# A decoder step on one core: two projections moved into the norm stage, one split around a product

## The chip, the cores and the metric
One Trainium2 chip, one of its cores. The metric is the time of one execution in microseconds (us) on the device, median of several runs. TensorE is called PE here, with PEld for its weight loads; VectorE is DVE, ScalarE is ACT, SyncE is SP (it issues most DMAs), GpSimd is POOL.

## The reference, cut to what matters
One layer of a decoder runs on 1024 prompt rows and 64 sampled rows (8 sequences of 8), each 1024 wide:

```python
h = rms_norm(x, norm_attn)
proj = h @ w_in                       # columns: x_r | q | k | v | gate a | gate b, each 1024 wide
x_c = causal_dwconv(x_r, ...)         # width 4
y_a = rg_lru(x_c, ...)                # gates, decay, a scan over positions
lam = exp(sum(lq1*lk1)) - exp(sum(lq2*lk2)) + lambda_init
# per head: w = softmax(q1 k1^T/8 + bias) - lam * softmax(q2 k2^T/8 + bias);  o = w v
y_b = rms_norm(o, subln_g) * (1 - lambda_init)
x = x + (sigmoid(g_a)*y_a + sigmoid(g_b)*y_b) @ w_out
h2 = rms_norm(x, norm_ffn)
x = x + (gelu(conv(h2 @ w_up)[:, :3072]) * conv(...)[:, 3072:]) @ w_down   # conv of width 3
y = rms_norm(x, norm_final)
```
The bias of a head depends only on the distance between query and key. The rows of K and V and several states are outputs too. Everything is float32; each large product is made of three products of rounded parts (high by high, high by low, low by high).

## The kernel before, in words
The program has four stages, one after another: `front`, `heads`, `sampled_and_out`, `mixer`. Each is a block in which every engine has its own list of instructions, tied together by semaphores. A block ends when all engines are through their lists; only then does the next one start.

**`front` (lines 88 to 361)** works on nine tiles of rows (eight of 128, one of 64). For each tile ACT sums squares and takes the root (`ssq`), DVE scales (`gain`), PE transposes eight 128x128 pieces into PSUM (`tile`, line 212), ACT writes the high part `h_hi` (`high`, 267), DVE the low part `h_lo` (`low`, 324). Transposes of tile t wait for `low` of tile t-2. Between tiles PE does four small things: transposes of parameter rows `prow` (222), three products that make the bias rows (229), one that spreads lambda over the partitions (234), and after tiles 6, 7 and 8 transposes of the mixer's parameter rows `frow` (244). DVE copies the bias rows to SBUF (343), SP writes them to DRAM (186). When ACT has done the high parts of the K and Q weights of head 0 (279), it issues two DMAs from DRAM to DRAM that lay these rows out as tiles: head 0 (283) and heads 1 to 7 (286). SP loads the weight slices `w_raw` of head 0 (180): K and Q behind all of x, V and XR behind the write of the bias rows.

**`heads` (445 to 1227)** runs over eight heads. All engines follow one list, `TURN` (364): each engine does its own part of every entry. `("P", g, c)` is the projection of group g (XR, K, Q, V, gates) for column chunk c (384, 384 and 320 columns): 24 matmuls (line 1152); `QK` are the scores, `SA`, `EX`, `SB` the softmax, `TW` transposes of the weights, `PV` the product with V (1220), `SQ` and `SS` the head's norm, `TR` transposes of K or V rows for the outputs (1179), `G..` the recurrent branch, `FA`, `FG` the merge. `P`, `TR`, `TW` and `G` results share three PSUM banks as a ring, taken in the order of `TURN`: an entry waits until the one three places before it has been released by ACT or DVE. `SA` of query block 0 needs the bias tile: SP waits for DMA 283, then loads it (693). At the start of the stage ACT and DVE split the V weights (711, 898), compute decay rates, split the XR weights, and split the small gate weights `rg_raw`, which SP loads at the stage's start (639).

PE's stage code ends a head with:
```python
("GAM",), ("P", GB, 1), ("P", GB, 2), ("TR", V_, 2), ("TW", 7, 0), ("TW", 7, 1), ("W", Q_, 1), ("TR", K_, 2),
("PV", 3), ("SQ", 3), ("FA",), ("SS", 3), ("FG",),
```
`("PV", 3)` is the last product with V; ACT then squares it (871) and copies it (872), and `("SQ", 3)` is PE's sum of the squares (1226).

Of the kernel before, what the change touches and what calls it, by code (L numbers as in the profile page):

```python
# [21 lines left out]
H, HD = 8, 64  # L22
# [64 lines left out]

def front(nc, sb, sem, ins, c):
# [13 lines left out]
    lam = sb("lam", [1, 4, HD], F32)  # L102
    lprod = sb("lprod", [1, 2, HD], F32)
    lsum = sb("lsum", [1, 2], F32)
    lexp = sb("lexp", [1, 2], F32)
    ltmp = sb("ltmp", [1, 2], F32)
    ones_row = sb("ones_row", [1, 128], F32)
# [29 lines left out]
    s_lsum = sem("s_lsum")  # L137
    s_lexp = sem("s_lexp")
    s_nl = sem("s_nl")
    s_nlb = sem("s_nlb")  # L140
# [6 lines left out]
    with nc.Block() as block:  # L147
        @block.sync
        def _(sp):
# [3 lines left out]

            load_x(0)
            sp.dma_start(g[:, :], broadcast_row(ins["norm_attn"], 128)).then_inc(g_in, 16)
            sp.dma_start(c.ptab[:, :], ins["page_table"].rearrange("(o b) n -> o (b n)", o=1)).then_inc(ptab_in, 16)
            for i, name in enumerate(("lambda_q1", "lambda_k1", "lambda_q2", "lambda_k2")):
                sp.dma_start(lam[:, i, :], ins[name]).then_inc(lam_in, 16)
# [8 lines left out]
            sp.dma_start(prow[r:r + n, :], flat(ins["state_rglru_conv"])).then_inc(prm_in, 16)  # L167
            load_x(3)
# [7 lines left out]
            sp.dma_start(frow[0:FCONV_W, :], flat(ins["ffn_conv_w"])).then_inc(frow_in, 16)  # L176
            sp.dma_start(frow[FCONV_W:FCONV_W + 1, :], flat(ins["ffn_conv_b"])).then_inc(frow_in, 16)
            sp.dma_start(frow[FCONV_W + 1:FROW, :], flat(ins["state_ffn_conv"])).then_inc(frow_in, 16)
            def load_w(grp):
                sp.dma_start(c.w_raw[:, W_SLOT[grp], :, :], c.w_in[:, :, COL0[grp]:COL0[grp] + 128])\  # L180
                  .then_inc(c.raw_in[W_SLOT[grp]], 16)

            load_w(K_)
            load_w(Q_)
            sp.wait_ge(rows_sb, 1)
            sp.dma_start(c.bias_rows_dram, bias_rows[:, :]).then_inc(rows_out, 16)
            load_w(V_)
# [4 lines left out]
            sp.wait_ge(rows_out, 16)  # L192
# [11 lines left out]
        def _(pe):  # L204
            def tile(t):
                n, u = rows(t), t % 2
                pe.wait_ge(xn_done, t + 1)
                for q in range(2):
                    if t >= 2:
                        pe.wait_ge(lo_done, 2 * (t - 2) + q + 1)  # L210
                    for k in range(4):
                        last = pe.transpose(ps[:, 2 * u + q, 128 * k:128 * k + n],
                                            xn[0:n, u, 512 * q + 128 * k:512 * q + 128 * (k + 1)],
                                            c.ident[0:n, 0:n])
                    last.then_inc(xt_done, 1)

            pe.wait_ge(id_done, 1)
            tile(0)
            tile(1)
            pe.wait_ge(prm_in, 16 * 7)  # L220
            for k in range(KT):
                last = pe.transpose(ps[:, 4, NROW * k:NROW * (k + 1)], prow[:, 128 * k:128 * (k + 1)],
                                    c.ident[0:NROW, 0:NROW])
            last.then_inc(prm_t, 1)
            tile(2)
            pe.wait_ge(tab_in, 32)
            pe.wait_ge(fills, 3)
            for i in range(3):
                last = pe.matmul(ps[0:H, 5 + i, 0:UW], rel[:, :], oh[:, UW * i:UW * (i + 1)],
                                 start=True, stop=True)  # L230
            last.then_inc(rows_mm, 1)
            tile(3)
            pe.wait_ge(s_nl, 1)
            pe.matmul(ps[:, 4, 480:481], ones_row[:, :], ltmp[:, 1:2], start=True, stop=True).then_inc(s_nlb, 1)
            tile(4)
            tile(5)
            half = DFF // 128
            pe.wait_ge(rows_sb, 1)
            for t in range(6, NT):
                tile(t)  # L240
                if t == 6:
                    pe.wait_ge(frow_in, 48)
                for k in range(16 * (t - 6), 16 * (t - 5)):
                    last = pe.transpose(ps[:, 5 + k // half, FROW * (k % half):FROW * (k % half + 1)],
                                        frow[:, 128 * k:128 * (k + 1)], c.ident[0:FROW, 0:FROW])
                last.then_inc(fprm_t, 1)

        @block.scalar
        def _(act):
            act.wait_ge(s_lsum, 1)  # L250
            act.activation(lexp[:, :], lsum[:, :], ACT.Exp).then_inc(s_lexp, 1)
            act.wait_ge(eps_set, 1)

# [9 lines left out]
            def high(t):  # L263
                n, u = rows(t), t % 2
                for q in range(2):
                    act.wait_ge(xt_done, 2 * t + q + 1)
                    act.activation(c.h_hi[:, 4 * q:4 * q + 4, 128 * t:128 * t + n],
                                   ps[:, 2 * u + q, :].rearrange("p (k n) -> p k n", k=4)[:, :, 0:n],
# [8 lines left out]
            for grp in (K_, Q_):  # L277
                act.wait_ge(c.raw_in[W_SLOT[grp]], 16)
                act.activation(c.w_hi[:, W_SLOT[grp], :, :], c.w_raw[:, W_SLOT[grp], :, :], ACT.Copy)\
                   .then_inc(c.whi_done[grp], 1)  # L280
            act.wait_ge(rows_out, 16)
            u0 = U0 - (BW - 256)
            act.dma_start(c.bias_tiles_dram[0].rearrange("p (a n) -> a p n", a=2), bass.AP(
                tensor=c.bias_rows_dram.tensor, offset=u0, ap=[[BW // 2, 2], [-1, 128], [1, BW // 2]]))\
               .then_inc(c.tile0_out, 16)
            act.dma_start(c.bias_tiles_dram[1:H], bass.AP(
                tensor=c.bias_rows_dram.tensor, offset=NU + u0, ap=[[NU, H - 1], [-1, 128], [1, BW]]))\
# [3 lines left out]
        def _(dve):  # L291
# [10 lines left out]
            dve.memset(ones_row[:, :], 1.0).then_inc(fills, 1)  # L302
            dve.memset(c.ones[:, :], 1.0).then_inc(fills, 1)

            dve.wait_ge(lam_in, 64)
            link(dve.tensor_tensor(lprod[:, :, :], lam[:, 0:4:2, :], lam[:, 1:4:2, :], ALU.mult))
            dve.reduce_sum(lsum[:, :], lprod[:, :, :], mybir.AxisListType.X).then_inc(s_lsum, 1)
            dve.wait_ge(g_in, 16)
# [11 lines left out]
            def low(t):  # L320
                n, u = rows(t), t % 2
                for q in range(2):
# [3 lines left out]
                        ps[:, 2 * u + q, :].rearrange("p (k n) -> p k n", k=4)[:, :, 0:n],  # L326
# [4 lines left out]
            for t in range(NT):  # L331
# [3 lines left out]
                if t == 1:  # L335
                    dve.wait_ge(prm_t, 1)
                    link(dve.tensor_copy(c.prm[:, :, 0:NROW],
                                         ps[:, 4, 0:NROW * KT].rearrange("p (k r) -> p k r", k=KT)))
                    link(dve.tensor_scalar(sp_t[:, 5, :], a_view, -1.0, None, ALU.mult))
                    link(dve.tensor_tensor(sp_t[:, 0, :], sp_t[:, 5, :], a_view, ALU.max))  # L340
                if t == 2:
                    dve.wait_ge(rows_mm, 1)
                    dve.tensor_copy(bias_rows[:, :].rearrange("h (i n) -> h i n", i=3), ps[0:H, 5:8, 0:UW])\
                       .then_inc(rows_sb, 1)
                    dve.wait_ge(s_lexp, 1)
                    link(dve.tensor_tensor(ltmp[:, 0:1], lexp[:, 1:2], lexp[:, 0:1], ALU.subtract))
# [98 lines left out]
def heads(nc, sb, sem, ins, outs, c):  # L445
# [165 lines left out]
    with nc.Block() as block:  # L611
# [92 lines left out]
        def _(act):  # L704
# [9 lines left out]
            if W_AHEAD[V_]:  # L714
                split_w(0, V_)
# [1852 lines left out]
```

## Time and profile before

| | us |
|---|---|
| median of 3 runs | 2152.4 (2152.14 to 2154.1) |
| the profiled execution | 2153.99 |
| its span, first to last instruction | 2152.2 |
| PE busy in the span | 2063.6 (96%) |
| DVE, ACT busy | 1409.7 (66%), 1004.9 (47%) |
| first projection on PE begins at | 50.5 |

The profile lists the engines' busy times, the DMA queues (q1 is SP's queue, q10 that of ACT), the chain of work that ended last, and the costliest groups. L1152 is line 1152 of the kernel. "Idle before" is the time that an engine stood still ahead of an instruction, with what ended it. Times within the trace count from the start of the span.

### The profile page before, as it was taken

What the parts mean: (1) busy time and instruction counts of PE and PEld (TensorE: products, weight loads), DVE (VectorE), ACT (ScalarE), POOL (GpSimd) and SP (SyncE); (2) the same over time, 40 slices, a digit from 0 to 9 for tenths busy, and PEclk for the clock granted to TensorE, in tenths of its full rate; (3) what the DMA queues carried; (4) which work ended last, traced back from release to release, by engine and by line L of the source; (5) the groups of instructions that cost most, each with busy time, mean ns of one, the idle gap of its engine ahead of it and who ended that gap; (6) DMA issues with size and microseconds to landing.
All of it is one profiled execution on the core that took longest, in us unless ns stands there. A gap on an engine that the chain in (4) does not pass through costs nothing. (4 is left out here: it accounts for less than half of the span.)

```text
span 2152.2 us, 36781 instructions
## 1 busy us (share of the span) xinstructions
PE 2063.6 (96%) x12238; PEld 1909.4 (89%) x12238; DVE 1409.7 (66%) x3014; ACT 1004.9 (47%) x1807; POOL 2.8 (0%) x8
## 2 busy tenths in 40 slices
PE   5999999999999999799999989999999999999998
PEld 4989999989999999688887879898989898989896
DVE  6676766766676767577775538474747474747476
ACT  5575656666575756566675324131313131313133
POOL 0000000000000000000000000000000000000000
PEclk9999999999999999899999999999999999999999
DMA  6321111111111112667664322020202020202012
GB/s 174 132 68 46 59 44 59 53 54 50 53 50 53 51 55 86 245 238 276 244 234 150 103 58 69 21 70 16 73 15 71 16 70 19 69 21 69 21 50 94
DMA packets 165021, 182.95 MB, mean 85 GB/s; under 512 B 10390, under 2 KB 136918, under 8 KB 164903
## 3 DMA queue, kind: packets, MB, share of 16 engines
q1 hardware_dynamic: 163762, 177.10, 25.6%
q10 hardware_dynamic: 1161, 4.72, 0.6%
q8 instruction: 40, 0.66, 0.1%
q14 instruction: 58, 0.48, 0.1%
HBM read 162.58 MB, written 24.46 MB: 87 GB/s over the span
## 5 line engine op out<-in xcount | busy, mean ns | idle before, releaser
L1152 PE MATMUL ps<-h_hi,w_hi 128*128 128x384 f32 (+1 forms) x1152 | 384.6, 334 | 7.5 <-DVEq L893 7.5
L1152 PE MATMUL ps<-h_hi,w_lo 128*128 128x384 f32 (+1 forms) x1152 | 376.7, 327 | 0.0
L1152 PE MATMUL ps<-h_lo,w_hi 128*128 128x384 f32 (+1 forms) x1152 | 376.3, 327 | 0.0
L2152 PE MATMUL ps<-h_hi,f_w_hi 128*128 128x320 f32 (+1 forms) x1136 | 371.6, 327 | 4.6 <-DVE f_w_lo L2291 4.1
L2152 PE MATMUL ps<-h_hi,f_w_lo 128*128 128x320 f32 (+1 forms) x1136 | 371.0, 327 | 0.0
L2152 PE MATMUL ps<-h_lo,f_w_hi 128*128 128x320 f32 (+1 forms) x1136 | 370.8, 326 | 0.0
L2126 PE MATMUL ps<-d_hi,act 128*128 128x512 f32 x816 | 257.0, 390 | 1.6 <-DVE d_lo L2330 1.6
L2228 ACT ACTIVATE yc<-ps,f_prm 128x384 f32<-128x384 f32 x144 | 93.5, 654 | 328.8 <-PE ps L2152 158.4
L1152 PEld LDWEIGHTS ps<-h_hi,w_hi 128*128 128x128 f32 x1152 | 217.0, 188 | 9.7 <-DVEq L893 7.6
L2152 PEld LDWEIGHTS ps<-h_hi,f_w_hi 128*128 128x128 f32 x1136 | 213.8, 188 | 5.2 <-DVE f_w_lo L2291 4.4
L1152 PEld LDWEIGHTS ps<-h_lo,w_hi 128*128 128x128 f32 x1152 | 217.1, 188 | 0.4
L1152 PEld LDWEIGHTS ps<-h_hi,w_lo 128*128 128x128 f32 x1152 | 216.8, 188 | 0.0
L2152 PEld LDWEIGHTS ps<-h_lo,f_w_hi 128*128 128x128 f32 x1136 | 213.8, 188 | 0.0
L2152 PEld LDWEIGHTS ps<-h_hi,f_w_lo 128*128 128x128 f32 x1136 | 213.7, 188 | 0.0
L2281 DVE TENSOR_TENSOR x<-x,ps 128x512 f32<-128x512 f32 x144 | 97.7, 686 | 140.9 <-PE ps L2126 138.3
L2126 PEld LDWEIGHTS ps<-d_hi,act 128*128 128x128 f32 x816 | 153.2, 188 | 33.9 <-DVE d_lo L2330 1.8
L2126 PE MATMUL ps<-d_lo,act 128*128 128x512 f32 x432 | 168.2, 389 | 0.0
L2352 DVE SCALAR_TENSOR_TENSOR yc<-ps,f_prm,yc 128x383 f32<-128x383 f32 x144 | 82.3, 571 | 101.9 <-ACT yc L2228 98.3
L1093 DVE CUSTOM_DVE_ANT_0 E<-ps,bias 128x256 f32<-128x256 f32 (+3 forms) x128 | 100.0, 818 | 31.6 <-PE ps L1196 31.0
L2178 ACT ACTIVATE f_st_rows<-ps 18x768 f32<-18x768 f32 x8 | 6.4, 799 | 234.4 <-PE ps L2090 234.4
L854 ACT ACTIVATE E<-E,nmx 128x256 f32<-128x256 f32 (+3 forms) x128 | 105.0, 824 | 17.0 <-DVE nmx L1097 11.9
L1789 DVE TENSOR_TENSOR kt_lo<-ps,kt_hi 128x512 fp32r<-128x512 f32 x128 | 82.6, 684 | 32.9 <-ACT kt_hi L1653 32.5
(286 smaller groups left out, 3728.9 us busy)
## 6 DMA issues: line engine op xcount, KB each, us to landing
k<-in_cache_k SPq DMA_DIRECT2D x64, 512.0 KB, 5.8
v_raw<-in_cache_v SPq DMA_DIRECT2D x64, 512.0 KB, 4.6
w_raw<-in_w_in SPq DMA_DIRECT2D x48, 512.0 KB, 4.1
f_raw<-in_w_up SPq DMA_DIRECT2D x48, 512.0 KB, 4.1
f_raw<-in_w_down SPq DMA_DIRECT2D x24, 512.0 KB, 3.5
bias<-bias_tiles_dram SPq DMA_DIRECT2D x8, 576.0 KB, 3.8
merged_dram<-mg SPq DMA_DIRECT2D x8, 544.0 KB, 2.7
xt<-in_x_prompt SPq DMA_DIRECT2D x8, 512.0 KB, 6.8
```

Source lines behind the costliest of these rows:

```text
L854: act.activation(E[i][:, 0:n], E[i][:, 0:n], ACT.Exp, bias=nmx[:, i:i + 1], accum_out=den[:, i:i + 1]).then_inc(exp_done, 1)
L1093: dve.tensor_tensor_reduce(out=E[i][:, 0:n], in0=S[i][:, 0:n], in1=bias[:, c0:c0 + n], scale=1.0, scalar=-3e38, op0=ALU.add, op1=ALU.max, ...
L1152: last_ = pe.matmul(bank(s)[:, 0:n], w[:, W_SLOT[g], k, :], x[:, k, off:off + n], start=(k == 0 and i == 0), stop=(k == KT - 1 and i == 2))
L1789: dve.tensor_tensor(kt_lo[:, h % 2, keys], tb[hf], kt_hi[:, h % 2, keys].bitcast(F32), ALU.subtract).then_inc(ktlo_done, 1)
L2126: l_ = pe.matmul(ps[:, down_bank(e), :], a, w[:, j, 512 * hf:512 * (hf + 1)], start=(j == 0 and i == 0), stop=(j == GF - 1 and i == len(pa ...
L2152: l_ = pe.matmul(ps[:, e % 6, 0:n], w[:, p, k, :], x[:, k, off:off + n], start=(k == 0 and i == 0), stop=(k == KT - 1 and i == 2))
L2178: act.activation(st_rows[:, :, :], ps[0:NST, b:b + 2, 0:128 * GF], ACT.Copy).then_inc(str_done, 1)
L2228: act.activation(yc[:, e % 3, 0:n], ps[:, e % 6, 0:n], ACT.Identity, bias=prm[:, p, FCONV_W:FCONV_W + 1], scale=prm[:, p, FCONV_W - 1:FCON ...
L2281: dve.tensor_tensor(x2, x2, ps[:, down_bank(e), :], ALU.add).then_inc(add_done, 1)
L2352: link(dve.scalar_tensor_tensor(out=y[:, 1:np_], in0=x[:, 0:np_ - 1], scalar=w[1], in1=y[:, 1:np_], op0=ALU.mult, op1=ALU.add))
```

## The change
There are two parts.

In `front`: PE computes the K and Q projections of head 0, chunk 0, there (`first_projection`): K in three parts after tiles 6, 7 and 8, then Q. For this the tiles' PSUM banks move from 0..3 to 2..5, and the ring's banks 0 and 1 take the two results. The mixer's parameter rows go in front of tiles 2, 3 and 4, the bias rows' products behind tile 4; their copies to SBUF move from DVE to ACT. SP loads the `frow` rows ahead of x tile 3, the K weights ahead of x tile 5; it waits for the bias rows' write itself, issues the layout DMA of head 0 on its own queue, and loads the V and XR weights behind it. ACT splits K, Q and V, and then issues the layout DMA of heads 1 to 7. Lambda is computed on all partitions, partly in `heads`. ACT preloads the table for the square root first.

```diff
+            sp.dma_start(frow[FCONV_W + 1:FROW, :], flat(ins["state_ffn_conv"])).then_inc(frow_in, 16)
             load_x(3)
...
             load_x(4)
+            load_w(K_)
             load_x(5)
...
+            for i, name in enumerate(("lambda_q1", "lambda_k1", "lambda_q2", "lambda_k2")):
+                sp.dma_start(lam[:, i, :], broadcast_row(ins[name], 128)).then_inc(lam_in, 16)
             for t in range(6, NT):
                 load_x(t)
...
             load_w(Q_)
             sp.wait_ge(rows_sb, 1)
             sp.dma_start(c.bias_rows_dram, bias_rows[:, :]).then_inc(rows_out, 16)
+            sp.wait_ge(rows_out, 16)
+            u0 = U0 - (BW - 256)
+            sp.dma_start(c.bias_tiles_dram[0].rearrange("p (a n) -> a p n", a=2), bass.AP(
+                tensor=c.bias_rows_dram.tensor, offset=u0, ap=[[BW // 2, 2], [-1, 128], [1, BW // 2]]))\
+              .then_inc(c.tile0_out, 16)
             load_w(V_)
             load_w(XR)
...
 PE's list:
             tile(0)
             tile(1)
+            param_rows()
+            mixer_rows(0, 16)
             tile(2)
+            mixer_rows(16, 32)
             tile(3)
+            mixer_rows(32, 48)
             tile(4)
+            bias_row_sums()
             tile(5)
+            tile(6)
+            first_projection(K_, range(0, 3))
+            tile(7)
+            first_projection(K_, range(3, 6))
+            tile(8)
+            first_projection(K_, range(6, KT))
+            first_projection(Q_, range(0, KT))
+            pe.wait_ge(first_done, 2)
...
 ACT's list, behind high(t):
+                if t == 3:
+                    act.wait_ge(fprm_t, 3)
+                    act.activation(fprm[:, :].rearrange("p (a n) -> p a n", a=2), ps[:, 0:2, 0:DFF // 128 * FROW],
+                                   ACT.Copy).then_inc(fprm_sb, 1)
+                if t == 4:
+                    split_w(K_)
+                if t == 5:
+                    act.wait_ge(rows_mm, 1)
+                    ...
+            split_w(Q_)
+            split_w(V_)
             act.wait_ge(rows_out, 16)
             act.dma_start(c.bias_tiles_dram[1:H], ...
```
`bias_row_sums` waits for the copies of the parameter rows (`prm_sb`, `fprm_sb`), `first_projection` for `low` of tile 2, the low part of its weights and the copy of the bias rows.

In `heads`: `("TR", K_, 2)` stands between `("P", GB, 1)` and `("P", GB, 2)`, no longer behind `("TW", 7, 1)`. PE's K projection of chunk 0 for the next head is done at the end of the head before, half ahead of `("PV", 3)` and half ahead of `("SQ", 3)`; in head 0 the K and Q projections of chunk 0 are left to `front`. The other engines keep their order.

```diff
-            def body(f, last):
+            def body(f, first, last):
                 for s in TURN:
+                    if s == ("PV", 3) and not last:
+                        project(f + 1, ("P", K_, 0), range(0, KT // 2))
+                    if s == ("SQ", 3) and not last:
+                        project(f + 1, ("P", K_, 0), range(KT // 2, KT))
+                    if s[0] == "P" and s != ("P", K_, 0) and not (first and s == ("P", Q_, 0)):
+                        project(f, s, range(0, KT))
...
-            turns(pe, body)
+            body(0, True, False)
+            with pe.Fori(1, H - 1) as f:
+                body(f, False, False)
+            body(H - 1, False, True)
```

## Rows read from the trace of the kernel before

**Rows 1.** The page, part 1: busy us (share) xinstructions of each engine.
```profile
PE 2063.6 (96%) x12238; PEld 1909.4 (89%) x12238; DVE 1409.7 (66%) x3014; ACT 1004.9 (47%) x1807; POOL 2.8 (0%) x8
```
**Rows 2.** Windows (stretch, us, busy, PEclk, DMA share, GB/s): tiles, and head 1.
```profile
14.00:42.00 28.00, 26.66 (x129) 20.12 (x129) 24.56 (x44) 19.06 (x40) 0.00 (x0) 1.00 0.82 176
...
156.10:259.50 103.40, 100.42 (x650) 94.71 (x650) 70.98 (x152) 64.52 (x121) 0.00 (x0) 1.00 0.18 54
```
**Rows 3.** Timeline of PE (start, us, line, operation, count, idle before): first 65 us.
```profile
17.76 1.07 PE L222 MATMUL ps<-ident,prow 40*128 40x40 f32 x8
18.93 1.97 PE L212 MATMUL ps<-ident,n_xn 128*128 128x128 f32 x8
20.83 4.49 PE L229 MATMUL ps<-oh,rel 33*8 33x432 f32 x6
...
34.52 1.89 PE L244 MATMUL ps<-ident,frow 20*128 20x20 f32 x16
...
50.51 0.69 PE L1152 MATMUL ps<-h_hi,w_hi 128*128 128x384 f32 x1 [7.52 <-DVEq L893]
...
53.88 0.52 PE L1152 MATMUL ps<-h_lo,w_hi 128*128 128x384 f32 x1
...
60.70 0.33 PE L1152 MATMUL ps<-h_hi,w_hi 128*128 128x384 f32 x1
...
64.95 0.39 PE L1196 MATMUL ps<-k_hi,q_hi 64*128 64x256 f32 x2
```
**Rows 4.** Timeline of ACT and its queue: end of front, start of heads.
```profile
41.21 1.25 ACTq L283 DMA_DIRECT2D bias_tiles_dram<-bias_rows_dram  x1
...
42.51 6.42 ACTq L286 DMA_DIRECT2D bias_tiles_dram<-bias_rows_dram  x1
49.88 1.06 ACT L711 ACTIVATE w_hi<-w_raw 128x1024 fp32r<-128x1024 f32 x1 [6.41 <-DVE xe L884]
...
58.24 0.42 ACT L742 ACTIVATE rg_hi<-rg_raw 128x256 fp32r<-128x256 f32 x1 [1.89 <-DMA rg_raw<-in_rg_w_x]
58.56 0.47 ACT L754 ACTIVATE k_hi<-ps 128x384 fp32r<-128x384 f32 x1
```
**Rows 5.** Waits of SP, 40 to 70 us: total, times, longest.
```profile
SPq L693 <- DMA bias_tiles_dram<-bias_rows_dram: 7.6, 1, 7.6
```
**Rows 6.** Timeline of DVE: the copy of the bias rows.
```profile
25.35 1.50 DVE L343 COPY bias_rows<-ps 8x1296 f32<-8x1296 f32 x1 [0.36 <-PE ps L229]
```
**Rows 7.** DMA issues (KB, us from issue to landing): x tile 2, x tile 7, V weights, bias tile.
```profile
xt<-in_x_prompt SPq DMA_DIRECT2D x1, 512.0 KB, 5.5
...
xt<-in_x_prompt SPq DMA_DIRECT2D x1, 512.0 KB, 14.7
...
w_raw<-in_w_in SPq DMA_DIRECT2D x1, 512.0 KB, 5.6
...
bias<-bias_tiles_dram SPq DMA_DIRECT2D x1, 576.0 KB, 7.1
```
**Rows 8.** DMA queues (packets, MB, share of 16 engines): 20:27, 43:49, 58.2:61.2, 79.2:84 us.
```profile
q1 hardware_dynamic: 422, 0.69, 100.5%
...
q10 hardware_dynamic: 88, 0.20, 10.3%
...
q10 hardware_dynamic: 121, 0.56, 44.9%
...
q10 hardware_dynamic: 55, 0.25, 12.7%
```
**Rows 9.** Timeline of PE and DVE where head 0 ends.
```profile
148.60 1.13 PE L1206 MATMUL ps<-ident,E 128*128 128x128 f32 x8
150.75 0.52 PE L1179 MATMUL ps<-ident,kvf 128*128 128x128 f32 x3 [1.02 <-issue]
...
155.34 0.70 PE L1226 MATMUL ps<-sq,ones 128*128 128x256 f32 x2 [0.75 <-ACT oT L872]
...
150.22 0.42 DVE L1074 TENSOR_TENSOR v_lo<-ps,v_hi 128x256 fp32r<-128x256 f32 x1 [1.02 <-ACT v_hi L842]
```

More of the change, by code:

```diff
@@ L215, in tile, with param_rows, mixer_rows, bias_row_sums @@
                     last.then_inc(xt_done, 1)
+            def param_rows():
+                pe.wait_ge(prm_in, 16 * 7)
+                for k in range(KT):
+                    last = pe.transpose(ps[:, 6, NROW * k:NROW * (k + 1)], prow[:, 128 * k:128 * (k + 1)],
+                                        c.ident[0:NROW, 0:NROW])
+                last.then_inc(prm_t, 1)
+            def mixer_rows(k0, k1):
+                half = DFF // 128
+                pe.wait_ge(frow_in, 48)
+                for k in range(k0, k1):
+                    last = pe.transpose(ps[:, k // half, FROW * (k % half):FROW * (k % half + 1)],
+                                        frow[:, 128 * k:128 * (k + 1)], c.ident[0:FROW, 0:FROW])
+                last.then_inc(fprm_t, 1)
+            def bias_row_sums():
+                pe.wait_ge(tab_in, 32)
+                pe.wait_ge(fills, 1)
+                pe.wait_ge(fprm_sb, 1)
+                pe.wait_ge(prm_sb, 1)
+                for i in range(3):
+                    last = pe.matmul(ps[0:H, ROW_BANKS[i], 0:UW], rel[:, :], oh[:, UW * i:UW * (i + 1)],
+                                     start=True, stop=True)
+                last.then_inc(rows_mm, 1)
+            def first_projection(grp, ks):
+                at = (K_, Q_).index(grp)
+                if ks[0] == 0:
+                    pe.wait_ge(lo_done, 6)
+                    pe.wait_ge(c.wlo_done[grp], 1)
+                    pe.wait_ge(rows_sb, 1)
+                for k in ks:
+                    for i, (w, x) in enumerate(((c.w_hi, c.h_hi), (c.w_hi, c.h_lo), (c.w_lo, c.h_hi))):
+                        last = pe.matmul(ps[:, at, 0:384], w[:, W_SLOT[grp], k, :], x[:, k, 0:384],
+                                         start=(k == 0 and i == 0), stop=(k == KT - 1 and i == 2))
+                if ks[-1] == KT - 1:
+                    last.then_inc(first_done, 1)
             pe.wait_ge(id_done, 1)
@@ L219, in _, with split_w @@
             tile(1)
[L220 to L224, printed above, removed]
-            tile(2)
[L226 to L231, printed above, removed]
+            param_rows()
+            mixer_rows(0, 16)
+            tile(2)
+            mixer_rows(16, 32)
             tile(3)
-            pe.wait_ge(s_nl, 1)
-            pe.matmul(ps[:, 4, 480:481], ones_row[:, :], ltmp[:, 1:2], start=True, stop=True).then_inc(s_nlb, 1)
+            mixer_rows(32, 48)
             tile(4)
+            bias_row_sums()
             tile(5)
[L237 to L246, printed above, removed]
+            tile(6)
[6 more added lines that the diff above has]
+            pe.wait_ge(first_done, 2)
         @block.scalar
         def _(act):
-            act.wait_ge(s_lsum, 1)
-            act.activation(lexp[:, :], lsum[:, :], ACT.Exp).then_inc(s_lexp, 1)
+            act.preload_act_table_set("sqrt_and_others")
             act.wait_ge(eps_set, 1)
+            def split_w(grp):
+                act.wait_ge(c.raw_in[W_SLOT[grp]], 16)
+                act.activation(c.w_hi[:, W_SLOT[grp], :, :], c.w_raw[:, W_SLOT[grp], :, :], ACT.Copy)\
+                   .then_inc(c.whi_done[grp], 1)
             def ssq(t):
@@ L392 @@
 RING, TRS, TWS = indices()
+assert RING["P", K_, 0] == 0 and RING["P", Q_, 0] == 1
 NSLOT = 3
@@ L718, in _ @@
             act.activation(c.sp_t[:, 1, :], c.sp_t[:, 0, :], ACT.Exp, scale=-1.0).then_inc(sp_act, 1)
+            act.activation(c.lexp, c.lsum, ACT.Exp).then_inc(sp_act, 1)
             act.wait_ge(sp_dve, 1)
```

154 lines of the change are left out of this document (66 added, 88 removed).

## The prediction
> **What bounds the kernel now.** I read the page first: PE is busy 96% of the span [rows 1], so time can only come from where PE stands still, from work taken out of it (none is here), or be lost where it is made to stand still. The table by stage puts the largest hole near the start: PE works through the norm's tiles up to 42 us [rows 2] and stands idle 7.52 us until its first projection at 50.51 [rows 3]. The timeline of ACT says why: PE's own list is long done, but the block ends only when ACT has finished issuing the layout DMA of heads 1 to 7, which holds its queue from 42.51 to 48.93; PE starts 1.58 us later [rows 3, 4]. Behind the block the first scores (QK 0) start at 64.95, after 72 matmuls of projections [rows 3]. In the heads a period is 103.4 us [rows 2], and its end shows two stalls of PE, in every one of the eight heads alike: 1.02 us ahead of the last K transposes, and 0.75 us ahead of the sum of squares, which waits for ACT's square and copy of the last product [rows 9]. Everything after the heads is untouched; it only shifts.
>
> **Change in the heads.** (a) The sum of squares: 12 matmuls of the next K projection (some 2.1 us at 0.177 us, from 24 in 4.25 us [rows 3]) now stand between the product and it. ACT needs less than 1 us for its two operations, so this stall goes. The product's 24 matmuls end in pitch near 154.4 and the sum starts at 155.34: 0.75 to 0.9 us each, 7 boundaries, 6.0 us. (b) The 1.02 us stall ends when DVE has released the ring's bank behind the V transposes, at 150.64 [rows 9]. Moving the K transposes up takes them out of that wait, but the first half of the next K projection needs exactly the same bank (it is the third ring entry after the V transposes), so it is late in their place: ACT and DVE handle the V transposes as long after PE as now. Gain nothing. (c) The last head has no next projection: its product with V then meets the release of the weight transposes by itself, some 0.5 us more. (d) SP now passes the K rows and states before the XR weight load, about 2 us later; those weights are needed over 6 us later. Later SS and merge: ACT and DVE reach the next head's K and Q parts about 3 us later, while PE has Q and V projections (8.5 us) ahead of QK 0. Hidden, with about 1.5 us to spare; without that cover it would cost the excess per head. Heads: -6.0 + 0.5 = -5.5 us.
>
> **Change in the front, PE.** 48 matmuls leave the heads' start. In the front they are free only if they fit in time that was idle. Removed at the start are also a table load and the wait for lambda, about 3 us, but what follows uses it up: PE's first mixer rows stand ahead of tile 2 and need all `frow` rows (480 KB, 24 KB to a partition). Call their landing F. Tile 2 of x landed 5.5 us after issue, 12.0 us, and now about 11; the rows queue behind it. A floor is 13 us (they cost next to nothing). For the other end: while they moved, 20 to 27 us, all 16 engines were busy and brought 0.69 MB in 7 us [rows 8], and x tile 7 took 14.7 us against 5.5 [rows 7], 9.2 us more. I take 11 + 9.2, F = 20.2; bounds 14 and 22. From there PE's list alone gives the bias rows: three times 16 small transposes at 1.83, tiles 2 to 5 at 1.9, the products 4.4 [rows 3]: F + 17.5; ACT's high part 0.7 and its two copies 1.5, as DVE's single one [rows 6]: R = F + 19.7 = 39.9. Before, R was 26.85.
> PE's own end: tiles 6 to 8, 4.9 us; K 24 matmuls at the slow pace of 0.34 (50.51 to 53.88 [rows 3]), 8; Q, waiting some 1.5 us for its weights' low part, 6 us: F + 38, 58 us.
>
> **Change in the front, the queues.** This decides. SP writes the rows at R, waits until they have landed (some 2.8 us, an estimate; bounds 2 and 4), issues the layout DMA of head 0 at 42.7, and only then loads V's weights, on the same queue. That DMA took from 41.21 until SP's wait for it ended at 58.39, 17.2 us [rows 4, 5]. The rows on queue 10 show how: 10.3% of 16 engines at 43 to 49 us, two engines at most; 44.9%, seven, once head 0's tile is done; 12.7%, two, at the end, when the other five are through [rows 8]. So the small tile is carried by two engines, each of these serves its own queue in order, and what was queued behind lags on these two alone. V's slice is spread over all 16, two of which first have the tile to carry. It lands not 5.6 us after its issue [rows 7] but behind the tile: 42.7 + 17.2 + 2 = 61.9. ACT splits it (1.06 [rows 4]), 63.0, and only then issues the layout DMA of heads 1 to 7: 6.42 us [rows 4] (lower bound 4.4, by head 0's 1.25 us for 256 of its pieces against 896; 6.42 taken, its own row): 69.4. PE starts 1.58 later: 71.0.
> The Trainium skill bears on this in "DMA: Bandwidth & Descriptors", "Why a DMA increments its semaphore by 16 and not by 1": HWDGE takes the largest number of engines up to 16 that divides the slowest dimension of both patterns, so 2 and 7 here; the trace agrees (10.3% and 44.9%). Its section "Queues, rings and completion order" has descriptors taken in ring order on each engine, which is what the lag of two engines shows.
>
> **From there to the scores.** PE meets the V projection at 71.0; before it was at 60.70 [rows 3]. It takes 6 instead of 4.25 us at the slow start, 77. But the K and Q results wait for ACT and DVE: ACT's k_hi began 9.6 us after the issue ended (48.93 to 58.56 [rows 4]), behind the gate weights' landing; without that wait 7.2. Low parts of K and Q 2.4 us more: QK 0 at 79.0 to 81.4, against 64.95: +14 to +16.4, taken +15.
>
> **Sum.** +15 - 5.5 = +9.5 us on the profiled 2153.99: 2163.5. The median is 1.6 below that execution: 2162 us.
>
> **Rivals.** (1) Order on the ring doesn't hold V up (its packets pass the tile's, or the tile goes faster on SP's queue). Then V is there at 50, ACT's issue ends at 58 to 60, with PE's own 58; QK 0 at 68.2 to 70.7. The tile lands at 59.9, the bias load begins after the block, at 60, and takes 7.1 [rows 7]: no earlier. +4.5 - 5.5: -1, 2151.5. For it: nothing but that both queues are not alike for certain; against it [rows 8]. It decides from the point at which V lands before PE's end (58). (2) The `frow` rows land early, F = 14: all of the front moves up by 6: +3.5, 2156. For it: with no x behind them, fewer transfers compete. Against: the stretch from 20 to 27 us. (3) Both at once: the front no longer than before, its 48 matmuls given back, and the boundaries' gain on top: -7, 2145.5. (4) The ring's wait at the boundary also vanishes (the release came earlier in the new order): 7 more us off the forecast, 2155.
> A change that does nothing is excluded by the moved matmuls.
>
> **How the numbers follow.** Forecast 0.58, its own range 2156 to 2167. Rival 1: 0.13, rival 2: 0.10, rival 3: 0.12, rival 4: 0.07. From no change this kernel's measurement tells about 0.2%, 4.3 us. Slower: all of the forecast and part of 2 and 4, 0.64. Same: rival 1 and the rest of 2 and 4, 0.20. Faster: 0.16. Range 2149 to 2167: it leaves out rival 3 and a front later than bounded.
>
> **What would show it.** PE's idle time ahead of the V projection grows from 7.5 us to over 10, and ends near 71; SP's DMA of head 0's tile is issued near 43; the V weights' landing time reads 17 to 20 us; ACT's DMA issue begins after 60. Mixer rows on PE begin near 20, with an idle gap before them. At the boundaries the 0.75 us in front of line 1226 is gone, and some 1.0 us stands in front of the K projection instead of line 1179. Wrong: V's landing within 8 us of issue; a first projection in the heads before 62; no idle gap ahead of the mixer rows.

## The result, and the profile after

The changed kernel takes 2156.34 us in the median of 20 runs (2153.86 to 2160.34); the kernel before, run beside it on the same chip, 2153.26 (2150.2 to 2156.94, 20 runs). The ratio is 1.0016, 95% interval 1.0009 to 1.0023: 3.1 us slower, inside the 0.2% that the prediction called no change. The forecast was 2162 and "slower", its range 2149 to 2167. So the time lies in the range and the call was wrong. That it lies no further from the forecast is partly luck: two terms of the sum were wrong by 6.5 and 3.8 us in the same direction, and 3.6 us that the sum had put at nothing went the other way. All ratios compare fast executions only; one of the 11 runs of experiment 10 took 3373.47 us at a granted clock of 0.567 and stands in none (without it the median there is 2153.86).

The profiled execution took 2156.73 us. Line 1187 of the new kernel is what line 1152 was (projections), 1241 is 1196 (QK), 1224 is 1179 (TR), 1265 and 1271 are 1220 and 1226 (PV, SQ). The page's first part, as [rows 1]: PE is 3.6 us less busy, in a span 2.7 us longer.

```profile
PE 2060.0 (96%) x12236; PEld 1909.5 (89%) x12236; DVE 1407.1 (65%) x3010; ACT 1005.5 (47%) x1809; POOL 2.8 (0%) x8
```

**The front.** The timeline of PE (start, us, line, operation, count, idle before):

```profile
21.49 1.89 PE L231 MATMUL ps<-ident,frow 20*128 20x20 f32 x16 [4.54 <-DMA frow<-in_state_ffn_conv]
...
53.16 0.34 PE L255 MATMUL ps<-h_hi,w_lo 128*128 128x384 f32 x1
63.53 0.66 PE L1187 MATMUL ps<-h_hi,w_hi 128*128 128x384 f32 x1 [10.03 <-DVEq L927]
...
73.48 0.38 PE L1241 MATMUL ps<-k_hi,q_hi 64*128 64x256 f32 x2 [3.06 <-DVE k_lo L1018]
```

The mixer's rows kept PE waiting until 21.49. PE's own list ended at 53.5, then it stood for 10.03 us (7.52 before, [rows 3]); the first scores came at 73.48 instead of 64.95, 8.5 us later. The timeline of ACT and its queue says what PE stood for, as [rows 4] did:

```profile
22.37 1.06 ACT L295 ACTIVATE n_junk<-xt 128x1024 f32<-128x1024 f32 x1 [6.46 <-DMA xt<-in_x_prompt]
...
59.50 1.06 ACT L289 ACTIVATE w_hi<-w_raw 128x1024 fp32r<-128x1024 f32 x1 [11.88 <-DMA w_raw<-in_w_in]
59.50 1.40 ACTq L329 DMA_DIRECT2D bias_tiles_dram<-bias_rows_dram  x1
62.16 1.28 ACT L751 ACT_TABLE_LOAD   x1 [1.61 <-PEq L144]
70.72 0.42 ACT L776 ACTIVATE rg_hi<-rg_raw 128x256 fp32r<-128x256 f32 x1 [3.06 <-DMA rg_raw<-in_rg_w_x]
```

ACT waited 11.88 us for V's weights and split them at 59.5. The layout DMA of heads 1 to 7 went out beside that split in 1.40 us, not in the 6.42 of [rows 4], and was through at 60.90. The last work of the block was DVE's low part of the same weights, until 61.81; 0.7 us later DVE began the next stage, and PE 1.7 us later. The timeline of DVE:

```profile
60.59 1.22 DVE L351 TENSOR_TENSOR w_lo<-w_raw,w_hi 128x1024 fp32r<-128x1024 f32 x1 [11.37 <-ACT w_hi L289]
```

The timeline of SP shows the queue that held the weights: behind the layout DMA of head 0 the issue of V's and XR's slices took 10.91 us.

```profile
40.94 0.30 SPq L183 DMA_DIRECT2D bias_rows_dram<-bias_rows  x1
42.90 0.74 SPq L186 DMA_DIRECT2D bias_tiles_dram<-bias_rows_dram  x1
43.69 10.91 SPq L152 DMA_DIRECT2D w_raw<-in_w_in  x2
```

Queue q1 shows how V came to be late: its share of 16 engines was 8.4% at 43 to 49 us (the tile alone), then 88.5% at 50 to 52 us, while 0.52 MB passed, and 16.7% at 52 to 54. V's own issue took until 49.1. By the volume, most of one slice of 512 KB was through by 52 (an inference); V's last part came at 59.5.

**The heads.** The table by stage for head 1 (stretch, us, busy of PE, PEld, DVE, ACT, POOL, granted clock, DMA share, GB/s) gives 101.96 us where [rows 2] has 103.40:

```profile
157.50:259.46 101.96, 99.79 (x651) 94.73 (x650) 70.93 (x152) 64.35 (x121) 0.00 (x0) 1.00 0.18 55
```

And the timeline of PE where head 1 and head 7 end, as [rows 9]:

```profile
261.32 0.44 PE L1187 MATMUL ps<-h_hi,w_hi 128*128 128x384 f32 x1 [0.97 <-DVE v_lo L1109]
...
268.48 0.59 PE L1271 MATMUL ps<-sq,ones 128*128 128x256 f32 x2
...
873.51 0.39 PE L1265 MATMUL ps<-wt_hi,v_hi 128*128 128x256 f32 x1 [1.59 <-DVE wt_lo L1149]
...
877.39 0.70 PE L1271 MATMUL ps<-sq,ones 128*128 128x256 f32 x2 [0.75 <-ACT oT L906]
```

The sum of squares no longer waits; a stall of 0.97 stands ahead of the K projection; in the last head, which has no next projection, the product waits 1.59 us. From QK 0 of head 0 to the last SQ the heads take 803.9 us, 9.3 less than before (64.95 to 878.20, now 73.48 to 877.39).

**Behind the heads.** From the last SQ to the end of the span: 1273.98 us before, 1277.54 now, though this code is unchanged. Windows of both kernels, one stretch of 30 us and the whole stretch behind the heads: first before, then after.

```profile
998.00:1028.00 30.00, 28.61 (x192) 25.91 (x191) 22.19 (x41) 20.02 (x40) 0.00 (x0) 1.00 0.74 263
...
878.90:2152.20 1273.30, 1230.76 (x6911) 1128.84 (x6910) 812.88 (x1733) 461.41 (x796) 2.05 (x2) 0.99 0.29 97
```

```profile
998.00:1028.00 30.00, 28.25 (x180) 25.56 (x179) 20.52 (x38) 18.18 (x37) 0.00 (x0) 0.94 0.70 245
...
878.00:2154.90 1276.90, 1231.19 (x6911) 1129.12 (x6910) 813.67 (x1733) 461.45 (x796) 2.05 (x2) 0.99 0.29 97
```

A granted clock of 0.94 over 30 us is 0.06 x 30 / 0.5 = 3.6 us at the 1.2 GHz level, which costs PE half of it, 1.8 us; the kernel before had none there. But elsewhere it had more (0.93 at 880 to 998 us, 0.94 after the change): over the whole stretch the clock reads 0.99 in both, and PE was busy only 0.4 us longer. So the clock explains little of the 3.6 us; some 3 us are time in which PE stood still. The balance of the profiled executions: +8.5 (front) - 9.3 (heads) + 3.6 (behind) = +2.8 us.

### The profile page after: what moved, and what is told of

It reads as the page before. It is cut to its first block and busy times, and to the rows that moved or that the text cites. A ratio compares the mean times of both kernels' runs of the same rounds, so it can differ in the third digit from the quotient of the medians.

```text
span 2154.9 us, 36749 instructions
## 1 busy us (share of the span) xinstructions
PE 2060.0 (96%) x12236; PEld 1909.5 (89%) x12236; DVE 1407.1 (65%) x3010; ACT 1005.5 (47%) x1809; POOL 2.8 (0%) x8
## 5 line engine op out<-in xcount | busy, mean ns | idle before, releaser
L1187 PE MATMUL ps<-h_hi,w_lo 128*128 128x384 f32 (+1 forms) x1136 | 371.7, 327 | 0.0
L1187 PE MATMUL ps<-h_lo,w_hi 128*128 128x384 f32 (+1 forms) x1136 | 371.4, 327 | 0.0
## 6 DMA issues: line engine op xcount, KB each, us to landing
xt<-in_x_prompt SPq DMA_DIRECT2D x8, 512.0 KB, 10.4
```

Of the source, the lines that this page charges most:

```text
L1187: last_ = pe.matmul(bank(s)[:, 0:n], w[:, W_SLOT[g], k, :], x[:, k, off:off + n], start=(k == 0 and i == 0), stop=(k == KT - 1 and i == 2))
```

## The experiments

Each was timed beside the kernel before on the same chip; medians of before were 2153.7, 2153.59 and 2152.9 in the three groups.

**1. The heads alone.** The kernel before with only the second half of the change:

```diff
+                    if s == ("PV", 3) and not last:
+                        project(f + 1, ("P", K_, 0), range(0, KT // 2))
+                    if s == ("SQ", 3) and not last:
+                        project(f + 1, ("P", K_, 0), range(KT // 2, KT))
```

> The kernel before with the change in the heads alone (K transposes moved up, next K projection split around the last product, PE's first head written out); the front and head 0's first K and Q projections stay as before. Theory A (the traces of both kernels: a head's period went from 103.4 to 101.95 us, 7 times 1.45, less 0.8 in the last head): -9.3 us against before, about 2144 us, a period near 101.95, the stretch behind the heads unchanged at about 1274 us. Theory B (the 3.6 us by which the stretch behind the heads was longer in the changed kernel belong to the new heads, say to PE's third copy of its code): -5.7 us, 2147.5, the stretch near 1277.5.

2144.43 us, ratio 0.9962 (0.9948 to 0.9975): 9.3 us faster, as expected. First scores at 64.55, period 101.95, 1273.40 us behind the heads. In this trace the way from the first scores to the last SQ is 8.6 us shorter than before. So the longer stretch behind the heads isn't brought by the new heads.

**2. The front alone.** The changed kernel with the old list of turns and the whole K projection at its old place.

```diff
-                    if s == ("PV", 3) and not last:
-                        project(f + 1, ("P", K_, 0), range(0, KT // 2))
-                    if s == ("SQ", 3) and not last:
-                        project(f + 1, ("P", K_, 0), range(KT // 2, KT))
```

> The changed kernel with the old order of the heads and the next K projection whole at its old place; the front is the new one, so head 0's first K and Q projections are still made there. Theory A (front costs 8.5 us, QK 0 at 73.5 instead of 64.95): +8.5 us against before, about 2162, period 103.4. Theory B as above: 2162 if the longer stretch behind the heads belongs to the heads, 2165.5 if it belongs to the front. Rival C (the front is nearly neutral, the loss is elsewhere): within 2 us of before.

2167.33 us, ratio 1.0059 (1.0046 to 1.0073): 13.6 us slower, 5 more than expected. Its trace has the first scores at 75.77 (2.3 later than with the whole change: SP waited 3.4 us instead of 1.6 for the write of the bias rows, and everything on its queue followed) and 1275.65 us behind the heads. Against before that is 10.8 us at the first scores, 1.0 in the heads and 1.7 behind them: theory A had the first too small and the other two at nothing. The mechanism is the same one: V's weights arrive late, the issue is short.

```profile
61.73 1.06 ACT L289 ACTIVATE w_hi<-w_raw 128x1024 fp32r<-128x1024 f32 x1 [13.49 <-DMA w_raw<-in_w_in]
61.74 1.39 ACTq L329 DMA_DIRECT2D bias_tiles_dram<-bias_rows_dram  x1
```

Front and heads alone add to 13.6 - 9.3 = +4.3, beside +3.1 for the whole.

**3. V's weights ahead of the layout DMA.** If V waits behind the small tile, load it in front.

```diff
             load_w(Q_)
+            load_w(V_)
+            load_w(XR)
             sp.dma_start(c.ptab, ...)
...
-            load_w(V_)
-            load_w(XR)
```

> The changed kernel with SP loading the V and XR weights right behind the Q weights, ahead of the bias rows' write and of head 0's layout DMA; nothing else. Theory A (the V weights' landing, held by the layout DMA on the two engines they share, sets the end of the front): V lands before 46 instead of 59.5, the block ends with PE's own 53.5, PE's first projection in the heads near 55 instead of 63.5; QK 0 near 65 instead of 73.5; the bias tile is then the last, landing at 67 to 70 instead of 73.5; 5 to 8 us below the changed kernel, 2148 to 2151. Rival D (ACT's issue of heads 1 to 7 then blocks for 5 us or more, as before): the block ends near 55.5, 2 us less gained. Rival E (the queue's order is not what held V): no change, 2156.

A miss: 2165.07 us, ratio 1.0052 (1.0038 to 1.0066), 8.7 slower than the changed kernel. ACT and PE did what was expected, and then PE stood 18.69 us ahead of the first scores:

```profile
47.12 1.39 ACTq L329 DMA_DIRECT2D bias_tiles_dram<-bias_rows_dram  x1
...
77.75 0.42 ACT L776 ACTIVATE rg_hi<-rg_raw 128x256 fp32r<-128x256 f32 x1 [15.90 <-DMA rg_raw<-in_rg_w_x]
```

```profile
57.39 0.41 PE L1187 MATMUL ps<-h_hi,w_hi 128*128 128x384 f32 x1 [1.63 <-DVEq L927]
80.52 0.58 PE L1241 MATMUL ps<-k_hi,q_hi 64*128 64x256 f32 x2 [18.69 <-DVE k_lo L1018]
```

The waits of SP name the cause (total, times, longest):

```profile
SPq L728 <- DMA bias_tiles_dram<-bias_rows_dram: 14.0, 1, 14.0
```

Head 0's tile, issued at 43.47, landed only at 71.4: 28 us instead of 17.2. In the kernel before both layout DMAs lie on ACT's queue, the small one first. Here they lie on two queues and go out 3.6 us apart, and the small one had to share its engines with the big one. (That they share them is inferred from this 28 and from experiment 4, where the small one is first on one queue with the big one, and lands 15.7 us after issue.) ACT can split K and Q results only behind the gate weights, whose load ended at 77.7 (20.7 us from issue) behind the same tile. V's late arrival had been protecting the tile. The Trainium skill says in "DMA: Bandwidth & Descriptors", "Queues, rings and completion order", that an engine takes turns between the queue rows it has work for, packet by packet; 28 us against 17.2 agrees with that.

**4. Head 0's tile back on ACT's queue**, right ahead of that of heads 1 to 7, the rest of the change kept.

```diff
             split_w(Q_)
+            act.wait_ge(rows_out, 16)
+            act.dma_start(c.bias_tiles_dram[0], ...).then_inc(c.tile0_out, 16)
             split_w(V_)
             act.wait_ge(rows_out, 16)
             act.dma_start(c.bias_tiles_dram[1:H], ...).then_inc(c.tiles_out, 16)
```

> The changed kernel with head 0's layout DMA issued by ACT on its own queue again, between the splits of Q and V, right ahead of that of heads 1 to 7; SP loads V and XR behind the bias rows' write. Theory A (ACT's 6.42 us issue in the kernel before was the queue behind its own small tile: both DMAs use the same two rings; in the changed kernel the small tile is on SP's queue and the issue took 1.40): the issue takes 5 us or more again, V lands within 8 us of its issue, the block ends near 55.5, the first projection of the heads is near 56; but the tile, issued near 47.5 and beside the large one, lands near 65, its load near 73: QK 0 near 65 to 67, SA 0 near 73; 0 to 3 us below the changed kernel. Rival F (the issue's length comes from the large DMA's own 896 runs): it would have to take about the same in all kernels; it is 1.40 in the changed one, so this rival expects 1.4 here.

2150.24 us, ratio 0.9983 (0.9973 to 0.9992). The timeline of ACT's queue settles what an issue costs:

```profile
46.46 1.25 ACTq L325 DMA_DIRECT2D bias_tiles_dram<-bias_rows_dram  x1
47.78 4.83 ACTq L329 DMA_DIRECT2D bias_tiles_dram<-bias_rows_dram  x1
```

The same DMA with the same pieces takes 4.83 us to issue behind the small tile, and 1.40 without it ahead on the queue. It is the queue that counts and not the engines: in experiment 3 the small tile was on its way too, but from SP's queue, and the issue took 1.39. V landed 4.8 us after its issue, the first scores came at 65.56. The block now ended with PE's own list (it stood for 1.63 us and went on at 55.33), so the longer issue cost nothing. Theory A had allowed 0 to 3 us below the changed kernel and it was 6.1; the tile had landed at 62.17 instead of 65.

**5. Head 0's tile in 16 pieces** of 72 columns instead of 2 of 576, otherwise the changed kernel.

```diff
-            sp.dma_start(c.bias_tiles_dram[0].rearrange("p (a n) -> a p n", a=2), bass.AP(
-                ..., ap=[[BW // 2, 2], [-1, 128], [1, BW // 2]]))
+            sp.dma_start(c.bias_tiles_dram[0].rearrange("p (a n) -> a p n", a=16), bass.AP(
+                ..., ap=[[BW // 16, 16], [-1, 128], [1, BW // 16]]))
```

> The changed kernel with head 0's layout DMA written as 16 column pieces of 72 instead of 2 of 576: 2048 runs of 288 bytes. Theory A (two engines carry it, 128 runs each; its 16.6 us hold V): with 16 engines it lands 3 to 7 us after its issue, V 1 to 2 us later, near 50; the block ends with PE, first projection of the heads near 55, the bias tile lands by 63; QK 0 near 65; 8 us below the changed kernel, 2148. Rival E (the number of engines isn't set by the outermost dimension, or DRAM writes of 288 bytes are slow): it takes 16 us or more, no gain, 2156 or worse.

2148.94 us, ratio 0.9983 (0.9974 to 0.9992): 7.4 faster than the changed kernel. The queue q1 at 43 to 49 us (packets, MB, share of 16 engines), the changed kernel first, then this one:

```profile
q1 hardware_dynamic: 73, 0.17, 8.4%
```

```profile
q1 hardware_dynamic: 2938, 1.03, 75.8%
```

The tile landed in 7.0 us, V in 8.1 and no longer 14 to 16; the first scores came at 65.47, 8 us earlier. The Trainium skill's rule in "DMA: Bandwidth & Descriptors", "Why a DMA increments its semaphore by 16 and not by 1" (the largest number up to 16 that divides the slowest dimension) gives 2 and 16 engines here; 8.4% and 75.8% agree.

**6. The heads alone, with 16 pieces.** Experiment 1 with the edit of experiment 5, on ACT's queue.

> The kernel before with the change in the heads alone, and head 0's layout DMA in 16 column pieces, still on ACT's queue. Theory A: the small tile lands 5 to 8 us after its issue at 41.2, the issue of heads 1 to 7 behind it takes 3 to 5 us instead of 6.4, the block ends near 47 and PE's first projection comes near 48.5 instead of 50.5; QK 0 is then set by the 72 matmuls, 63; 1 to 2.5 us below the kernel with the heads alone: 2142 to 2143.5. Rival: the 16 rings now all hold runs of the small tile, so the issue blocks as long, nothing is gained: 2144.5.

2144.85 us, ratio 0.9959 (0.9945 to 0.9972). The issues shrink from 1.25 and 6.42 us to:

```profile
41.26 0.72 ACTq L283 DMA_DIRECT2D bias_tiles_dram<-bias_rows_dram  x1
42.02 1.80 ACTq L286 DMA_DIRECT2D bias_tiles_dram<-bias_rows_dram  x1
```

The first projection comes 1.5 us earlier than in experiment 1 (47.70), QK 0 at 62.87 (1.7 earlier). Of the 5.2 us that left ACT's queue, 1.7 reach the scores: PE still stands 4.66 us between the stages, now because of its own last transposes of mixer rows, which DVE copies before it makes the low parts of the K and Q weights (the last thing in the front, until 46.50); and the gate weights land in 10.0 us. The median is the rival's 2144.5, but the rival's reason fails, as the issue took 1.80. The medians don't tell 1 and 6 apart: on the old front the 16 pieces gained nothing that can be measured.

**7. The mixer's rows spread over 120 partitions.** Experiment 5, and the rows in pieces of 4 KB, so that 8 transposes do for 48. The bias rows' copies also move ahead of the split of the K weights, which now comes behind tile 5.

```diff
-    frow = sb("frow", [FROW, 2 * DFF], F32)
+    frow = sb("frow", [6 * FROW, D], F32)
...
             param_rows()
-            mixer_rows(0, 16)
+            mixer_rows()
             tile(2)
-            mixer_rows(16, 32)
             tile(3)
-            mixer_rows(32, 48)
-            tile(4)
             bias_row_sums()
+            tile(4)
             tile(5)
```

> The changed kernel with head 0's layout DMA in 16 pieces and the mixer's parameter rows loaded as 120 partitions of 4 KB instead of 20 of 24 KB: 8 transposes instead of 48, ahead of tile 2; the bias rows' products then come behind tile 3. Theory A (PE's 4.5 us wait and ACT's 6.5 us wait for x tile 3 come from 24 KB runs into 20 partitions): the rows land by 15 instead of 21.4, x tile 3 lands by 17 instead of 22.3, PE has no gap above 1 us there, the bias rows are ready near 33 instead of 40.9, PE ends the front near 47 instead of 53.5; QK 0 near 59 to 60; 5 to 6 us below the kernel with 16 pieces: 2143. Rival G (x tile 3 is late through sheer volume on the queue): rows and x land 2 us earlier at most, 2147.

2145.91 us, ratio 0.9959 (0.9945 to 0.9973): 3 faster than experiment 5. The wait of 4.54 us at 21.49 is gone and the bias rows were written at 33.35 instead of 40.94, but most of that came back as other waits in the timeline of PE:

```profile
23.02 1.97 PE L214 MATMUL ps<-ident,n_xn 128*128 128x128 f32 x8 [2.63 <-DVE n_xn L362]
34.44 1.10 PE L214 MATMUL ps<-ident,n_xn 128*128 128x128 f32 x8 [1.59 <-DVE n_xn L362]
39.12 0.66 PE L255 MATMUL ps<-h_hi,w_hi 128*128 128x384 f32 x1 [3.59 <-issue]
...
64.60 0.58 PE L1242 MATMUL ps<-k_hi,q_hi 64*128 64x256 f32 x2 [5.65 <-DVE k_lo L1019]
```

The front's transposes wait for x, then the projection for the low part of its weights (DVE had it at 39.02, as the split had been moved back), and 5.65 us in front of the scores stay: the first scores move by 0.9 us only. Theory A's times for the rows held (by 16.8, ready at 33.35), its 59 to 60 for the scores did not. Another 1.2 us lie behind the heads (1274.33 against 1275.53).

**8. The layout DMA of heads 1 to 7 later.** Experiment 7, with this DMA issued by ACT in the prologue of `heads`, behind the SP loads that the first scores need.

> As the kernel with 120 rows, and ACT issues the layout DMA of heads 1 to 7 in the heads' stage, behind the decay rates' activations, no longer at the end of the front. Theory A (the gate weights' and the bias tile's loads are slowed by that DMA on seven shared engines: 9.2 and 10.3 us): both land within 5 us of issue, k_hi follows 6.5 us after the stage's start instead of 8.9, QK 0 comes 2 us earlier than without it: 2141. Rival: ACT's queue time for the issue, 1.4 us, falls on the path to k_hi and eats the gain.

2142.76 us, ratio 0.9947 (0.9933 to 0.9960): the fastest version, 10.8 us under the kernel before and 13.6 under the change. Its DMA issues (KB, us to landing), where experiment 7 has 10.2 for the bias tile and 9.2 for `rg_w_x`:

```profile
bias<-bias_tiles_dram SPq DMA_DIRECT2D x1, 576.0 KB, 4.0
...
rg_raw<-in_rg_w_x SPq DMA_DIRECT2D x2, 64.0 KB, 4.5
```

The wait ahead of the scores falls from 5.65 to 3.40 us, and they start at 62.60.

**9. The same without the two projections in the front:** experiment 6, with the layout DMA of heads 1 to 7 in the prologue of `heads`. The whole front is that of before, so this kernel lacks experiment 7's rows too.

> The front of before, the heads of after, head 0's layout DMA in 16 pieces, and the layout DMA of heads 1 to 7 issued by ACT only in the heads' prologue. Theory A: the two projections in the front are not what gains in e9_tiles_later; what gains there is the freed queue of ACT and freed engines. Then here ACT's queue ends the front 1.8 us earlier than in e7_heads_16 (its second issue took 1.80), the bias tile's load falls from 11.6 to 4-5 us, the first scores start at 60.5 to 61.5 (62.87 in e7, 62.60 in e9), and the median is 2142 to 2143, level with e9's 2142.76. Rival B: the 48 matmuls moved into the front are worth something once nothing else holds PE; then this one stays 1.5 us or more above e9: 2144.5 or more, first scores at 62.5 or later.

2143.63 us, ratio 0.9959 (0.9946 to 0.9973). Each interval just holds the ratio of the other (experiment 8: 0.9947, 0.9933 to 0.9960), and the profiled executions took 2142.83 and 2142.77: the new front, with the 48 matmuls and the 120 rows in it, has gained nothing that these runs can show, even with the queues clear. A gain of some 2 us is not excluded, and the new front without the two projections was not run. The timeline of PE shows the trade:

```profile
46.45 0.66 PE L1152 MATMUL ps<-h_hi,w_hi 128*128 128x384 f32 x1 [4.66 <-DVEq L893]
61.46 0.39 PE L1206 MATMUL ps<-k_hi,q_hi 64*128 64x256 f32 x2
```

From the first projection of the stage to the scores takes 15.0 us here and 7.8 in experiment 8 (54.79 to 62.60), 7.2 less; the stage's first projection comes 8.3 us later there. The scores start where theory A had them; the median, 1.1 us above the centre of A's range and 0.9 below B's bound, decides nothing by itself.

**10 and 11. Each half of the split by itself.** Experiment 1 with all 24 matmuls ahead of the product:

```diff
                     if s == ("PV", 3) and not last:
-                        project(f + 1, ("P", K_, 0), range(0, KT // 2))
-                    if s == ("SQ", 3) and not last:
-                        project(f + 1, ("P", K_, 0), range(KT // 2, KT))
+                        project(f + 1, ("P", K_, 0), range(0, KT))
```

> e1_heads_only, but all 24 matmuls of the next K projection ahead of the last product with V, none between it and the sum of squares. It prices the half behind the product. Theory A: the wait for ACT's square and copy is back in front of the sum (0.75 as in before) and with it the refill of the pipeline behind a stall; of the 1.45 us by which a head's period fell, 0.75 to 1.0 is lost again at 7 boundaries: 5.3 to 7 us over e1's 2144.4, so 2150 to 2151.5, with 1.0 us of stall still ahead of the K projection. Rival B: the gain came from moving the K transposes up, and the split is worth little: within 2 us of e1, 2146 or less.

and with all 24 behind it (the same line under `("SQ", 3)`):

> e1_heads_only, but all 24 matmuls of the next K projection behind the last product with V, ahead of the sum of squares. It prices the half ahead of the product. Theory A: the ring's wait ahead of the K projection goes (its bank is free by then), but the product itself now stands right behind the weights' transposes and waits for their low part, as it does in the last head (1.59 us there), 0.6 us more than the 1.02 that goes: 7 times 0.6, 4 us over e1's 2144.4, 2148 to 2149. Rival B: the product needs the transposes' low parts only in its later matmuls and starts at once; then both stalls are gone, 7 times 1.0 us less than e1: 2137 to 2138.

2154.29 us (ratio 1.0003, 0.9994 to 1.0012) and 2152.97 (1.0000, 0.9991 to 1.0009): in the medians all of it on either side gives the whole gain back, more than either theory said. In the traces a little stays: from the first scores to the last SQ 0.8 and 1.4 us less than before, where experiment 1 has 8.6. All ahead, head 1's end on PE:

```profile
255.59 0.44 PE L1152 MATMUL ps<-h_hi,w_hi 128*128 128x384 f32 x1 [0.97 <-DVE v_lo L1074]
...
263.63 0.70 PE L1234 MATMUL ps<-sq,ones 128*128 128x256 f32 x2 [0.75 <-ACT oT L872]
```

Both stalls of before are there; the period is 103.07 us, 1.12 more than in experiment 1 and 0.33 less than before. 0.75 to 1.0 had been foreseen for each boundary. Another 1.9 us lie in the front of this one execution (scores at 66.49), whose code is that of experiment 1; why, the trace doesn't tell. All behind, the timeline and a window of PE (clock 0.51):

```profile
254.01 0.38 PE L1228 MATMUL ps<-wt_hi,v_hi 128*128 128x256 f32 x1 [1.73 <-DVE wt_lo L1114]
```

```profile
254.80:258.20 3.40, 3.40 (x18) 3.40 (x17) 3.21 (x5) 1.09 (x1) 0.00 (x0) 0.51 0.71 207
```

The product waits 1.73 us for the weights' low part where the K projection waited 0.97: 0.76 for each of 7 heads, and the period is 102.67, 0.72 more than in experiment 1. In one head of seven the clock then fell to the 1.2 GHz level for 3.3 us, and that head took 1.53 us longer.

## Why the prediction came out as it did

**What held.** The front's chain, link by link, from [rows 3 to 8]: the mixer's rows at 21.5 (F = 20.2 said); the bias rows' write at 40.94 (39.9); head 0's layout DMA at 42.90 (42.7); V's weights at 59.5 (61.9), held up by the tile ahead of them on the queue, which experiments 4 and 5 show by taking the tile off that queue or spreading it over 16 engines; the stall of 1.02 moved in front of the K projection instead of vanishing (rival 4 refuted); the wait at the sum of squares gone; SP's reordering in the heads hidden; K and Q results waiting for the gate weights. Rival 1 (V not held up) fell. So did rivals 2 and 3: F was not 14. The last head lost 0.83 (0.5 said). PE's own list ended at 53.5 and not at 58: the sum had K's 24 matmuls 0.34 us apart, and they ran 0.18 apart at a granted clock of 1.00. That changed nothing here, since V's weights set the end of the block.

**The step that failed** is this one: "and only then issues the layout DMA of heads 1 to 7: 6.42 us (... 6.42 taken, its own row): 69.4." It took 1.40 us, began with the split and not behind it, and was not on the path at all. The lower bound of 4.4 scaled another issue in the same queue, and was no bound either. Experiments 3 and 4 show why: the length belonged not to the DMA, but to what stood on its own queue ahead of it. In [rows 4] that was head 0's tile, on two engines; the change itself had moved the tile to SP's queue. The same effect showed up there instead, as 10.91 us for V's and XR's slices; what it cost beside the wait on the two engines was not tested. Of the 7.5 us by which the V projection came earlier than the 71.0 said, 2.4 are the earlier landing of V and 5.2 this step: behind ACT's split came DVE's 1.25 us (to 61.81) and not an issue of 6.42; from there PE took 1.72 us to start, 0.1 more than said. From there to the scores 9.95 us passed, 8.0 to 10.4 were said; the scores came 8.5 us later than before, not 15.

**A term of the sum that was too small:** the heads. The sum had 6.0 us at 0.75 to 0.9 for each of 7 boundaries; measured 1.45, 10.2 in all. Experiment 10 prices the half behind the product: without it a period is 1.12 us longer, of which the trace shows 0.75 as idle time. The rest shows in the starts of the matmuls around the stall, in head 1: the sum starts 1.02 us behind the product's last matmul, where the product's own pitch is 0.12, and the third matmul of the next projection starts 1.13 us behind the sum, 0.78 in experiment 1. That a pipeline ran dry and filled again there is a reading of these numbers and not tested. The 0.33 that remain against before belong to the moved K transposes and the projection's new place together; no run parts the two. Nor are the halves' prices a sum: experiment 11 takes 0.72 for the other half, and 1.12 + 0.72 is more than 1.45. Idle time in front of an instruction was less than what the stall cost.

**What the prediction left at nothing:** the stretch behind the heads, +3.6 in the profiled execution. Over all 13 kernels it was 1272.7 to 1277.5 us. The six with the old front had 1273.6 in the mean (1272.7 to 1274.3), the seven with the new one 1275.6 (1274.2 to 1277.5). Each is the stretch of one execution, and executions of one kernel lie up to 6.7 us apart, so part of the 3.6 may be chance. The clock holds little of it, as the windows above say; what PE waited for longer, and why that should hang on the front, no run tells. That stays open.

The three together: -6.5, -3.8 and +3.6 against the forecast of 2163.5 for the profiled execution give its 2156.73. With the issue at 1.4 and a boundary at 1.45 the same working comes to 2162 - 5.0 - 4.2 = 2152.8 in the median, "no change" by the prediction's own 0.2%. Measured were 3.1 us more than before, clear of the noise but inside that 0.2%; the 3.6 us behind the heads would still have been missing.

## What to carry to other kernels

The time that an engine spends issuing a DMA depended here on what its queue still held (1.40 to 6.42 us for the same DMA); when a change moves the DMA ahead of it elsewhere, the old row is no estimate, and both must be asked: what stands ahead, and on how many engines. Ask too what else the block waits for: once the issue was short, DVE's low part ended the stage. The layout DMA with an outermost dimension of 2 ran on two engines and delayed what stood behind it; cutting it into 16 pieces gained 7.4 us with one line where V's weights stood behind it (experiment 5), and nothing measurable where they did not (experiment 6). And a piece of independent work can be worth most when it is split between two stalls: all of it at either one of them gained nothing in the median.

## What was not expected of the hardware

- A DMA of 4032 KB took 6.42, 4.83, 1.80 or 1.40 us to issue, by what stood ahead of it on its own queue.
- Between two queues a small DMA isn't served first: 28 us instead of 17.2 for 576 KB on two engines beside the big one.
- A stall with 0.75 us of idle time cost 1.12 us of period.
- Behind 10.03 us of standstill the first 17 matmuls of the stage ran at the 1.2 GHz level, here in a window of the changed kernel:

```profile
63.53:68.85 5.32, 5.32 (x17) 5.32 (x18) 3.98 (x19) 4.06 (x6) 0.00 (x0) 0.50 0.75 249
```

- A stall of 1.73 us was followed by that level in one head of seven, one of 0.97 in none.
